# Moving the norm's weighting of y and the last two pieces of the residual from VectorE to GpSimd

## What is computed

```
def rms_norm(x, w, eps=NORM_EPS):
    xf = x.astype(jnp.float32)
    y = xf * lax.rsqrt(jnp.mean(xf * xf, axis=-1, keepdims=True) + eps)
    return (y * w.astype(jnp.float32)).astype(x.dtype)
...
        h = h + rms_norm(mix, norm_post_mix[l])
        m = sq_relu_mlp(rms_norm(h, norm_pre_mlp[l]), mlp_w1[l], mlp_w2[l])
        h = h + rms_norm(m, norm_post_mlp[l])
```

## Time and profile before

| what | us |
|---|---|
| median of three runs | 2616.0 (2612.4 to 2617.43) |
| the profiled execution's own time | 2613.69 |
| its span, first to last instruction | 2611.8 |
| TensorE busy in the span | 2540.4 (97%) |
| VectorE busy | 1813.2 (69%) |
| ScalarE busy | 1213.0 (46%) |
| GpSimd busy | 151.7 (6%) |

### The profile page before, as it was taken

How to read it: one execution, slowest core, us unless ns; L and a number is a source line. 1 busy time by engine, 2 the same in 40 slices (tenths; PEclk the granted TensorE clock), 3 DMA queues, 4 the chain that set the end, 5 groups by cost and what they waited for, 6 DMA issues and landing times.

```text
span 2611.8 us, 46209 instructions
## 1 busy us (share of the span) xinstructions
PE 2540.4 (97%) x17290; PEld 2335.2 (89%) x17290; DVE 1813.2 (69%) x2643; ACT 1213.0 (46%) x1580; POOL 151.7 (6%) x269
## 2 busy tenths in 40 slices
PE   6999999999999999999999999999899999999997
PEld 6999999999888989898988888998699898989896
DVE  4878777877876565656666776777865656666666
ACT  4555545554554344444344554455444444343443
POOL 2222022202100000000000000000000000000000
PEclk9999999999999999999999999999899999999999
DMA  6665656656556666666666555565366666666664
GB/s 180 199 188 172 196 177 201 190 179 186 173 164 190 191 190 188 192 189 190 191 187 192 165 173 171 162 184 157 119 182 189 192 188 190 191 188 190 190 189 136
DMA packets 266505, 474.08 MB, mean 182 GB/s; under 512 B 16577, under 2 KB 50226, under 8 KB 264626
## 3 DMA queue, kind: packets, MB, share of 16 engines
q1 hardware_dynamic: 263296, 457.76, 58.5%
q0 software_dynamic: 2624, 15.00, 1.7%
q10 hardware_dynamic: 498, 0.18, 0.0%
HBM read 470.70 MB, written 2.19 MB: 181 GB/s over the span
## 4 chain that ended last, share of the span: by engine, by line
PE 84%; DVE 9%; ACT 3%; issue 2%; DMA 1%; POOL 0%; ACTq 0%; DVEq 0%; SPq 0%; POOLq 0%
PE ps L1272 27%; PE ps L1274 27%; PE ps L1273 27%; DVE whl L830 3%; ACT whl L573 1%; DVE conv L1082 1%; ACT junk L576 1%; DVE h L949 1%; PE ps L1441 1%; DVE stat L852 0%; DVE xhl L906 0%; DVE y L890 0%; DVE y L922 0%; DMA par_rows<-a_conv_b 0%; DVE stat L856 0%
## 5 line engine op out<-in xcount | busy, mean ns | idle before, releaser
L830 DVE TENSOR_TENSOR whl<-raw,whl 128x1024 fp32r<-128x1024 f32 x865 | 1073.7, 1241 | 732.9 <-ACT whl L573 719.4
L573 ACT ACTIVATE whl<-raw 128x1024 fp32r<-128x1024 f32 x865 | 916.4, 1060 | 1224.6 <-PE ps L1274 1214.2
L1272 PE MATMUL ps<-xhl,whl 128*128 128x256 f32 (+1 forms) x3600 | 1014.4, 282 | 10.9 <-DVE xhl L906 9.9
L1274 PE MATMUL ps<-xhl,whl 128*128 128x256 f32 (+1 forms) x3600 | 1006.6, 280 | 0.0
L1273 PE MATMUL ps<-xhl,whl 128*128 128x256 f32 (+1 forms) x3600 | 1004.9, 279 | 0.0
L1272 PEld LDWEIGHTS ps<-xhl,whl 128*128 128x128 f32 (+1 forms) x3600 | 677.2, 188 | 16.8 <-DVE xhl L906 11.6
L1273 PEld LDWEIGHTS ps<-xhl,whl 128*128 128x128 f32 (+1 forms) x3600 | 677.4, 188 | 3.1 <-issue 1.9
L1274 PEld LDWEIGHTS ps<-xhl,whl 128*128 128x128 f32 (+1 forms) x3600 | 677.0, 188 | 0.0
L1272 PE MATMUL ps<-whl,bhl 128*128 128x512 f32 x1376 | 538.9, 392 | 4.5 <-DVE y L890 2.9
L1273 PE MATMUL ps<-whl,bhl 128*128 128x512 f32 x1376 | 537.2, 390 | 0.0
L1274 PE MATMUL ps<-whl,bhl 128*128 128x512 f32 x1376 | 536.7, 390 | 0.0
(11 more groups left out here) (204 smaller groups left out, 1597.8 us busy)
## 6 DMA issues: line engine op xcount, KB each, us to landing
raw<-mlp_w SPq DMA_DIRECT2D x512, 512.0 KB, 4.2
raw<-a_in_proj SPq DMA_DIRECT2D x161, 512.0 KB, 4.5
raw<-a_out_proj SPq DMA_DIRECT2D x64, 512.0 KB, 4.0
raw<-b_w_q SPq DMA_DIRECT2D x32, 512.0 KB, 4.1
raw<-w_k SPq DMA_DIRECT2D x32, 512.0 KB, 3.7
raw<-w_v SPq DMA_DIRECT2D x32, 512.0 KB, 3.7
raw<-b_out_proj SPq DMA_DIRECT2D x32, 512.0 KB, 3.7
cumb<-cum_scratch POOLq DMA_DIRECT2D x8, 1024.0 KB, 7.7
```

The lines of the kernel that those rows point to most:

```text
L573: sc.activation(whi[:, s.split, :], raw[:, s.raw, :], ACT.Copy).then_inc(hi_ready, 1)
L830: ve.tensor_tensor(out=wlo[:, s.split, :], in0=raw[:, s.raw, :], in1=whi[:, s.split, :].bitcast(F32), op=ALU.subtract).then_inc(lo_ready, 1)
L1272: te.matmul(outs, lh, rh, start=start, stop=False, skip_group_check=True)
L1274: return te.matmul(outs, ll, rh, start=False, stop=stop, skip_group_check=True)
```

## The change

GpSimd takes over `weigh_y` for all four blocks at all four changes, and at the first three changes the pieces 3 and 4 of the residual (`residual_tail`), with two operations for each t in place of one: a scaling of y in place, then an addition of h. VectorE keeps pieces 0 to 2, and at the end all five. The pieces of h now count on two semaphores, `h_new` and `h_tail`, and the waits follow. GpSimd's new work stands ahead of the load of the next `postw`. In the rows of the programs' order below, line numbers of the rows called "now" are those of the changed file.

```diff
-H_STEPS = MT * len(H_PIECES)
+POOL_PIECES = (3, 4)
+H_HEAD, H_TAIL = 3 * MT, len(POOL_PIECES) * MT
...
+            def weigh_y(r):
+
+                pool.wait_ge(postw_in, 16 * (r + 1))
+                for nt in range(NT):
+                    pool.wait_ge(y_sq, MT * (NT * r + nt + 1))
+                    cols = slice(nt * BLK, (nt + 1) * BLK)
+                    g_.tensor_tensor(out=y[:, :, cols], in0=y[:, :, cols],
+                                     in1=postw[:, cols].unsqueeze(1).to_broadcast([P, MT, BLK]),
+                                     op=ALU.mult).then_inc(yw_ready, 1)
+
+            def residual_tail(r):
+
+                pool.wait_ge(h_new, H_HEAD * r + 1)
+                pool.wait_ge(yw_ready, NT * (r + 1))
+                for n in POOL_PIECES:
+                    lo, hi = H_PIECES[n]
+                    for t in range(MT):
+                        chain.mark(g_.tensor_scalar(y[:, t, lo:hi], y[:, t, lo:hi], rsy[:, t:t + 1], None, ALU.mult))
+                    for t in range(MT):
+                        chain.wait(back=1 - t)
+                        g_.tensor_tensor(out=h[:, t, lo:hi], in0=y[:, t, lo:hi], in1=h[:, t, lo:hi], op=ALU.add).then_inc(h_tail, 1)
+
             def next_postw(r, vec):
+                weigh_y(r - 1)
+                residual_tail(r - 1)
                 pool.wait_ge(yw_ready, NT * r)
...
+            weigh_y(3)
...
+                        if nt >= 2:
+                            act.wait_ge(y_sq, MT * (NT * r + nt - 1))
...
-                        act.wait_ge(h_new, H_STEPS * r)
+                        act.wait_ge(h_new, H_HEAD * r)
+                        act.wait_ge(h_tail, H_TAIL * r)
...
-            def weigh_early(r, i):
-
-                if i in (3, 5):
-                    weigh_y(r, i // 2 - 1)
...
-                weigh_y(r, 2)
                 dve.wait_ge(y_sq, MT * NT * (r + 1))
...
                 if slab:
                     split(slab)
-                residual(r, 3)
-                weigh_y(r, 3)
-                residual(r, 4)
+                    return
+                for n in POOL_PIECES:
+                    residual(r, n)
...
-                pe.wait_ge(h_new, H_STEPS * (r - 1) + MT * (1, 2, 3, 3, 4, 4, 5, 5)[i])
+                if i < 4:
+                    pe.wait_ge(h_new, H_HEAD * (r - 1) + MT * (1, 2, 3, 3)[i])
+                else:
+                    pe.wait_ge(h_tail, H_TAIL * (r - 1) + MT * (i // 2 - 1))
```

More of the change, by code:

```diff
@@ L322, in build @@
         y_sq, yw_ready, h_new, h_sq, rms_ready = sem("y_sq"), sem("yw_ready"), sem("h_new"), sem("h_sq"), sem("rms_ready")
+        h_tail = sem("h_tail")
         rows_cleared = sem("rows_cleared")
@@ L434, in _ @@
             for n, (lo, hi) in enumerate(H_PIECES):
-                sp.wait_ge(h_new, 3 * H_STEPS + MT * (n + 1))
+                sp.wait_ge(h_new, 3 * H_HEAD + MT * (n + 1))
                 sp.dma_start(out[0, :, lo:hi].rearrange("(t p) n -> p t n", p=P), h[:, :, lo:hi]).then_inc(stored, 16)
@@ L552, in _ @@
             pool.wait_ge(bias_out, 16)
-            pool.wait_ge(h_new, 2 * H_STEPS)
+            pool.wait_ge(h_new, 2 * H_HEAD)
             tab_load(0)
@@ L792, in att_step @@
                     if i >= 6:
-                        act.wait_ge(h_new, H_STEPS * 2)
+                        act.wait_ge(h_new, H_HEAD * 2)
+                        act.wait_ge(h_tail, H_TAIL * 2)
                         square_sums(2, range(4 * (i - 6), 4 * (i - 5)))
@@ L863, in diagonal, with steps @@
                     ve.tensor_scalar(dst[:, t, :], ident[:, :], rs[:, t:t + 1], None, ALU.mult).then_inc(done, 1)
-            def steps(ph, first_k, order, body, t=0, per=0, urgent=False, early=None):
+            def steps(ph, first_k, order, body, t=0, per=0, urgent=False):
                 for k, (unit, i) in enumerate(order):
                     ahead = ph.slab(first_k + k + LEAD, t, per)
-                    if early:
-                        early(unit, i)
                     if urgent and k == len(order) - 1:
@@ L915, in x_halves @@
                     x_half(i, TURN_BANKS[i], xhi, xlo, col, x_lo)
[L917 to L924, removed]
             def last_output(ph, i):
@@ L1126, in _ @@
             gate_factor(G)
-            steps(mix, 217, ACC, lambda u, i: last_output(mix, i), urgent=True, early=lambda u, i: weigh_early(0, i))
+            steps(mix, 217, ACC, lambda u, i: last_output(mix, i), urgent=True)
             boundary(0, mlp0.slab(LEAD - 1), 32)
@@ L1171, in mlp @@
                 chain.leave(7, 4)
-                steps(ph, 232, MLP_LAST, lambda u, i: last_output(ph, i) if u == "acc1" else step(u, i, 14), urgent=True,
-                      early=lambda u, i: weigh_early(r, i) if u == "acc1" else None)
+                steps(ph, 232, MLP_LAST, lambda u, i: last_output(ph, i) if u == "acc1" else step(u, i, 14), urgent=True)
             mlp(mlp0, 1, 32)
@@ L1258, in _ @@
                 attend(j, QG - 1, LAST_PLAN)
-            steps(att, 120, ACC, lambda u, i: last_output(att, i), urgent=True, early=lambda u, i: weigh_early(2, i))
+            steps(att, 120, ACC, lambda u, i: last_output(att, i), urgent=True)
             boundary(2, mlp1.slab(LEAD - 1), 48)
```

## The result

The changed kernel took **2626.8 us** in the median of five runs (2625.3 to 2628.1), the kernel before, on the same chip, 2615.1 (2612.4 to 2617.4): a ratio of 1.0046, 95% interval 1.0031 to 1.0061. It is slower by some 12 us. The profiled executions differ by 13.1 us in span (2624.9 against 2611.8).

What follows compares the result with a forecast made beforehand. TensorE was taken to stall at stage changes where VectorE is packed. Blocking by GpSimd and the slower clock, less relief, gave 3.5 + 2.65 + 2.65 and zero at the end: 8.8 us on 2616.0, 2625, range 2613 to 2633.

Steps and rivals of the forecast that it cites:

- Taken from VectorE: Weighings and h operations leaving VectorE at the changes and the end would gain 5.3 us if nothing else moved.
- Step (1): Third change, before the sum: splits wait for GpSimd's weighings, so the sum comes 0.95 us late; 2.0 at the first change.
- Step (2): Inverse root, third change: its first two-input step waits for weighing 3, 1.85 us more; first piece of h 2.8 late.
- Rival (b): Large operations block each other, one-element steps slip through: 2614.9 us; chance 0.24 together with (c) and mixtures inside the bound.
- Step (3): Third change: GpSimd's scalings fit into VectorE's 0.83 us idle before splitting x; TensorE's first step starts 2.8 late.
- Step (4): Third change, after the first step: third step possible after 7.7 us, not 9.20; 1.5 back, net 1.3 late.
- Step (5): TensorE's clock falls after 4.1 us idle, for 3.3 us, costing 1.65; third change 2.65 late.
- Rival (c): VectorE blocked, but the clock holds: 4.8 us slower, 2620.8; chance 0.24 together with (b) and mixtures inside the bound.
- The sum: Whole kernel: 3.5 + 2.65 + 2.65 and zero at the end, 8.8 us, put on the median 2616.0: 2625.
- Pieces 3 and 4 hidden: GpSimd's pieces ready at 1887.5 and 1894.1, TensorE asks at 1893 and 1896.7 (third change): costed at nothing.
- Rival (d): All prices at upper ends, weighings of 2.87 and longer slow clock: 2634 us; in the 0.62 with the forecast.
- Rival (a): The relief wins: blocking costs less than VectorE's freed work, gaining 5.3 us, 2610.7; chance 0.14.

Runs made afterwards that it cites:

- reorder_awake50: Kernel before, with block 3's weighing and piece 4 moved after x's second pair, and 50 instead of 40 filler transposes: 2609.0 us, 0.9983.
- weigh_early_pool: Kernel before, but GpSimd weighs blocks 0 and 1 only; VectorE keeps blocks 2 and 3 and all of h: 2620.5 us, 1.0022.
- probe_read: Kernel before plus six unused GpSimd products at each change, let go when the last squares are done, beside the inverse root: 2626.7 us, 1.0042.
- weigh_only: Changed kernel, but VectorE makes all five pieces of h; GpSimd only weighs all blocks: 2629.0 us, 1.0052 against the kernel before.
- awake75: Changed kernel with 75 instead of 40 filler transposes ahead of each stage: 2624.8 us, 1.0036 against the kernel before.
- tail_only: Changed kernel, but VectorE weighs all blocks as before; GpSimd only makes pieces 3 and 4: 2618.3 us, 1.0007 against the kernel before.

## Why the prediction was right

It said 2625, slower, within 2613 to 2633; the median is 2626.8. The profile of before held the mechanism, and each of its steps can be found in the trace after.

**Taken from VectorE: 5.3 us if nothing else moved.** Right in kind: the stall of 1.58 us before the third step is gone. `reorder_awake50`, which removes that stall at the changes without GpSimd, gives 2.9 us in span over the three changes (1.8, 0.8 and 0.3), against the 3.2 that I had put on the stalls of the first and third.

**Step (1), the blocked splits.** Two splits held, 2.21 and 2.51 us. The sum came 0.90 and 0.91 late at the third and second change (forecast 0.95), at the first 1.33 instead of 2.0. There VectorE idled 1.36 and 1.35 ahead of the two held splits, waiting for ScalarE, so its chain had the slack that I had denied it:

```profile
707.64 2.57 DVE L861 TENSOR_TENSOR whl<-raw,whl 128x1024 fp32r<-128x1024 f32 x1 [1.36 <-ACT whl L600]
714.14 2.52 DVE L861 TENSOR_TENSOR whl<-raw,whl 128x1024 fp32r<-128x1024 f32 x1 [1.35 <-ACT whl L600]
```

`weigh_early_pool` shows that this step, with the clock behind it, costs 5.5 us.

**Step (2), the inverse root.** Right that tiny instructions wait for a whole weighing, and that it ends with weighing 3. Wrong in which: I let the first two-input step wait, from 0.80 after the sum. It was a one-input scaling (L877), and the one at the root's head too, held for weighing 2. So the root lost 2.38, not 1.85, and at the first change 2.27, not 1.65. That the two-input steps are held as well, once their turn falls beside a GpSimd product, is shown by `probe_read`. Rival (b), that tiny steps slip through, is refuted by both. The Trainium skill, "SBUF — State Buffer", section "Who interferes with whom", led me to look for two inputs, and the trace agrees for the splits. The same section also says that `tensor_scalar` can contend with GpSimd when it runs in a mode that uses both of VectorE's ports, and that I passed over: the instructions held longest here, 2.27 us, were of this kind. Whether they ran in that mode no run shows.

**Step (3), the first step 2.8 late.** It was 3.75. The sum gave back 0.05. Of what is left, 0.53 are step (2)'s, and 0.47 lie between the first piece of h and the first step, 3.90 instead of 3.43. That is the clock, which was low already at the transposes (2.26 instead of 1.45) and which I let fall only at the step. It is not GpSimd's scalings: in `weigh_only`, without them and with the clock low, the distance is 3.90 too, and in `awake75`, with them and the clock up, it is 3.43.

**Step (4), the way back.** I let TensorE begin its third step 7.7 us after the first if the clock held. `awake75` shows 8.8 at the first and third change. I had costed GpSimd's scalings at 0.6 us, nearest to its copy, where they take 2.1 (1.55 at least), more than its two-input product of 1.29; in turns with them VectorE's two operations of piece 2 took 3.22 us, not 2.35, and TensorE waits 1.22 for this piece. In the changed kernel the slow step covers that wait.

**Step (5), the clock.** It fell at every change, as forecast, but for 6.8 to 10.2 us, not 3.3. At the third change the third step came 9.98 after the first (22.06 less 12.08), where I had 9.05, mostly because the first step took 5.28 and not 2.91 + 1.65 = 4.56. At the second it was 9.52, and at the first, where the slow stretch was the shortest, 8.94. At the third: 3.75 + 9.98 − 9.20 = 4.53, against 2.8 − 0.15 = 2.65. Rival (c), that the clock holds, is what `awake75` makes nearly true: 2.1 us cheaper by the medians, not 4, since the wait for piece 2 then comes to light.

**The sum.** First change 4.0 (forecast 3.5), second 4.0 (2.65), third 4.5 (2.65), the end 0.5 (zero; there the root was held 2.04, not 1.3): 13.1 in span against 8.8. The medians lie 11.8 apart. The forecast missed the median by 1.8 only, less than the 3.0 by which its sum fell short of that difference: partly luck, for I had added the sum to 2616.0, where the median of before is now 2615.1. The mechanism was right and its price too low. The mis-sized terms are the root's (0.5 to 0.6 a change), the slow transposes, which I had at nothing (0.47 a change), and the way from the first to the third step (0.9 at the third change, 0.5 at the second). At the first change the sum, 0.67 less late than forecast, made up for part of it.

**Pieces 3 and 4 hidden.** Right: no wait of TensorE for GpSimd's h stands in the trace after. But in `tail_only`, where TensorE starts on time and piece 4 must wait for VectorE's weighing of block 3, it is waited for (1.30 and 2.19). What hides it in the changed kernel, the late start or the weighings done early, no run isolates.

**Rival (d)**, weighings of 2.87, did not come: 2.38 us each, beside 2.40 taken from the earlier trace rows. Rival (a), the relief, is real in part: `reorder_awake50` shows that 2.9 us can be had. The delay of 3.3 to 3.6 us at each first piece of h buries it.

## What to carry to other kernels

Before moving work to an idle GpSimd, list what VectorE does in SBUF at that time, and do not take the smallest instructions for free: here sixteen tiny steps ahead of a waiting TensorE lost 2.0 to 2.4 us beside operations of 2.4 us, a split of 1.22 only 1.0 to 1.3. Where VectorE is the bound in a short stretch only, look first for its work that can stand a step later; and where TensorE idles ahead of that stretch, keep its clock up as well: each of the two repairs alone gained nothing that could be measured here, for the other loss took its place.

## What the runs showed that I had not expected

- A VectorE scaling of 128x2 numbers, one input, took 2.27 us instead of 0.17 beside GpSimd's weighing, and 0.60 beside GpSimd products of 0.67. Beside write-only clearings it took 1.31 at the second change and 0.20 at the first, with the same code. Two-input steps of 128x1 numbers were not held by the clearings beside them.
- GpSimd's scaling of 128x512 by one number a partition took 1.55 us at least and 2.1 in the mean; the product with that number repeated 512 times took 1.04 at least and 1.63 in the mean, and the addition of two full inputs 1.41 in the mean in the same kernel.
- With ten more filler transposes the kernel before keeps its clock and gains nothing (1.0001): a slow step of TensorE cost nothing as long as a stall of its own length stood behind it.
